# A hybrid decoder layer on one core: old recurrence states as the moving operand, a fourth PSUM place for y, two stores from GpSimd

## The reference

```python
def step(S, inp):
    qc, lfc, kc, vc = inp
    b = jnp.cumsum(lfc, axis=2)
    o_inter = jnp.einsum('bhtd,bhde->bhte', qc * jnp.exp(b), S)
    ...
    o = o_inter + jnp.einsum('bhts,bhse->bhte', A, vc)
    ...
    return S, o
```

```python
o = rmsnorm(o, out_g.reshape(HG_HEADS, HG_DV))
o = o * jax.nn.silu(hg.astype(jnp.float32).reshape(B, T, HG_HEADS, HG_DV))
```

## Time and profile before

| | us |
|---|---|
| median of three runs | 1187.14 (1183.54, 1187.14, 1187.34) |
| profiled execution, its time | 1183.51 |
| profiled execution, its span | 1181.7 |
| PE busy | 1137.4 (96%) |
| DVE busy | 571.8 (48%) |
| ACT busy | 442.9 (37%) |
| GpSimd busy | 354.6 (30%) |
| mean granted clock of TensorE | 0.991 |

### The profile page before, as it was taken

How to read it: one execution, slowest core, us unless ns; L and a number is a source line. 1 busy time by engine, 2 the same in 40 slices (tenths; PEclk the granted TensorE clock), 3 DMA queues, 4 the chain that set the end, 5 groups by cost and what they waited for, 6 DMA issues and landing times.

```text
span 1181.7 us, 20633 instructions
## 1 busy us (share of the span) xinstructions
PE 1137.4 (96%) x8955; PEld 1018.9 (86%) x8955; DVE 571.8 (48%) x788; ACT 442.9 (37%) x737; POOL 354.6 (30%) x226
## 2 busy tenths in 40 slices
PE   5999999999999999999999999999999999999997
PEld 4997564456799999889999877999999999999997
DVE  5533354767436664576622444854444444512332
ACT  6433455667452125222631343243333344311211
POOL 1332100210333163252033101433344444434441
PEclk9999999989999999999999999999999999999999
DMA  5443320420715251224673533323222232313311
GB/s 189 129 141 108 105 92 1 143 73 1 245 65 161 72 177 46 72 80 135 214 286 104 205 148 118 104 72 105 75 90 90 76 104 72 108 63 99 98 63 76
DMA packets 91394, 130.13 MB, mean 110 GB/s; under 512 B 6677, under 2 KB 78729, under 8 KB 89001
## 3 DMA queue, kind: packets, MB, share of 16 engines
q1 hardware_dynamic: 83448, 101.71, 26.3%
q0 software_dynamic: 7856, 27.11, 6.9%
HBM read 120.38 MB, written 12.59 MB: 113 GB/s over the span
## 4 chain that ended last, share of the span: by engine, by line
PE 87%; DVE 5%; ACT 3%; DMA 2%; issue 1%; SPq 0%; DVEq 0%; ACTq 0%
PE ring L742 47%; PE hold L844 6%; PE ring L714 5%; PE ring L1238 2%; PE ring L1437 2%; PE ring L1153 2%; PE ring L1252 2%; PE ring L939 2%; PE ring L950 2%; PE hold L970 1%; PE ring L789 1%; DMA arena<-in_cache_mem_v 1%; PE ring L1500 1%; PE ring L1386 1%; PE ring L1464 1%
## 5 line engine op out<-in xcount | busy, mean ns | idle before, releaser
L633 POOL TENSOR_TENSOR weight_lo<-w_ring,weight_hi 128x1024 fp32r<-128x1024 f32 (+1 forms) x108 | 264.0, 2445 | 551.7 <-ACT weight_hi L1705 551.6
L1705 ACT ACTIVATE weight_hi<-w_ring 128x1024 fp32r<-128x1024 f32 (+1 forms) x135 | 140.4, 1041 | 434.4 <-PE ring L742 358.6
L742 PE MATMUL ring<-operand_hi,weight_hi 128*128 128x272 f32 (+1 forms) x1056 | 219.2, 289 | 0.3 <-ACT arena L2008 0.3
L742 PE MATMUL ring<-operand_lo,weight_hi 128*128 128x272 f32 (+1 forms) x1056 | 218.7, 288 | 0.0
L742 PE MATMUL ring<-operand_hi,weight_lo 128*128 128x272 f32 (+1 forms) x1056 | 217.6, 287 | 0.0
L742 PEld LDWEIGHTS ring<-operand_hi,weight_hi 128*128 128x128 f32 (+1 forms) x1056 | 164.6, 187 | 3.9 <-issue 2.8
L742 PEld LDWEIGHTS ring<-operand_hi,weight_lo 128*128 128x128 f32 (+1 forms) x1056 | 164.7, 187 | 0.4
L742 PEld LDWEIGHTS ring<-operand_lo,weight_hi 128*128 128x128 f32 (+1 forms) x1056 | 164.5, 187 | 0.4
L844 PE MATMUL hold<-arena,w_ring 128*128 128x504 f32 (+1 forms) x192 | 77.2, 521 | 1.2 <-DVE arena L2376 1.2
L1685 ACT ACTIVATE arena<-ring 128x1024 f32<-128x1024 f32 (+8 forms) x75 | 55.5, 748 | 55.5 <-PE ring L742 16.7
L2829 DVE TENSOR_TENSOR x_res<-x_res,ring 128x544 f32<-128x544 f32 x24 | 17.3, 721 | 119.8 <-PE ring L742 119.5
(11 more groups left out here) (441 smaller groups left out, 2185.3 us busy)
## 6 DMA issues: line engine op xcount, KB each, us to landing
w_ring<-in_w_in SPq DMA_DIRECT2D x13, 1024.0 KB, 5.3
w_ring<-in_ffn_w_gate SPq DMA_DIRECT2D x11, 1024.0 KB, 5.3
w_ring<-in_ffn_w_up SPq DMA_DIRECT2D x11, 1024.0 KB, 5.3
w_ring<-in_ffn_w_down SPq DMA_DIRECT2D x8, 1024.0 KB, 5.1
arena<-in_cache_mem_k SPq DMA_DIRECT2D x6, 1024.0 KB, 8.4
arena<-in_cache_mem_v SPq DMA_DIRECT2D x5, 1024.0 KB, 12.1
w_ring<-in_ca_wk SPq DMA_DIRECT2D x4, 1024.0 KB, 5.1
w_ring<-in_ca_wv SPq DMA_DIRECT2D x4, 1024.0 KB, 5.4
```

Source lines behind the costliest of these rows:

```text
L633: self.ops.tensor_tensor(half_of(WL, self.x, kk, cols), w, half_of(WH, self.x, kk, cols).bitcast(F32), ALU.subtract).then_inc(sem("weights ...
L742: last = mm(ps[0:cols, hf * 512:hf * 512 + HALF], half_of((WH, WL)[pw], x, KT, cols)[:, i, :], (xh, xl)[px][:, k, hf * HALF:(hf + 1) * HAL ...
L1705: fn(half_of(WH, y, kk, cols), w, COPY).then_inc(sem("weights_hi"), 1)
```

## The change

Samples: `sample_outputs` on PE is new and runs before `hg_output(0)`. It makes the queries the stationary operand and the old states the moving one. For each head and sequence the stationary block has 32 columns, one per sample token, in which only the 4 columns of the sequence hold queries and the others zeros; DVE writes these blocks in `state_queries` (a memset and four copies into the free buffer `hK`). All 32 + 4 matmuls add up in `HOLD`, 32 rows by 512 columns, a new entry `so` of `hold`. ACT copies them to `orows`, and `hg_output` ends with one transpose of the head's 128 columns into the item, in the place of the nine matmuls.

Order: on ACT the last gate's sigmoid goes ahead of the four `mixed_hi`, on DVE `out_gate(3)` and `gates_ready` go ahead of the four `mixed_lo`. The squares of the memory rows go one head earlier on ACT; their scaling on DVE goes from ahead of `out_taken(3)` to behind the mean square of the outputs.

End: tile 2 of y goes to `HOLD`, and GpSimd issues the stores of tiles 1 and 3.

```diff
+Y_HELD = 2
...
-        item("y", tt)
+        if tt != Y_HELD:
+            item("y", tt)
...
-    hold += [("As",), ("osum",)] + [("rows", h) for h in range(HH)]
-    hold += [("dSs", h) for h in range(HH)] + [("cS",), ("cO",)]
+    hold += [("As",), ("so",), ("osum",)] + [("rows", h) for h in range(HH)]
+    hold += [("dSs", h) for h in range(HH)] + [("cS",), ("cO",), ("y",)]
...
+            def sample_outputs():
+
+                open_hold(("so",))
+                pe.wait_ge(sem("values_in"), 2)
+                pe.wait_ge(sem("state_queries"), HH)
+                for h in range(HH):
+                    hs = slice(h * HK, (h + 1) * HK)
+                    pe.wait_ge(sload[h], 16)
+                    for b in range(DB):
+                        mm(HOLD[0:NSMP, hs], qby[h][:, b, :], S0[:, h, b * HK:(b + 1) * HK],
+                           start=(h == 0 and b == 0), stop=False, skip_group_check=True)
+                    last = mm(HOLD[0:NSMP, hs], AS_[0:NSMP, h, :], hi[0:NSMP, QT, hs], start=False, stop=True,
+                              skip_group_check=True)
+                last.then_inc(hold_full, 1)
+
             def hg_output(h):
...
-                pe.wait_ge(sload[h], 16)
...
-                for b in range(DB):
-                    mm(ps[:, 512 + DS * b:512 + DS * b + DS], S0[:, h, b * HK:(b + 1) * HK],
-                       hQ[:, h, SEQ + DS * b:SEQ + DS * b + DS], start=(b == 0), stop=False, skip_group_check=True)
-                mm(ps[:, 512:TOK], hi[0:NSMP, QT, hs], AS_[0:NSMP, h, :], start=False, stop=True,
-                   skip_group_check=True).then_inc(psum_full, 1)
+                pe.wait_ge(hold_free, hold[("so",)] + 1)
+                tr(ps[:, 512:TOK], orows[:, hs], ident[0:NSMP, 0:NSMP]).then_inc(psum_full, 1)
...
-                evac(act, key)
-                sigmoid(hG[:, h, :], sem("gate_sigmoid"))
...
+            act.wait_ge(hold_full, hold[("so",)] + 1)
+            fn(orows, HOLD[0:NSMP, 0:HH * HK], COPY).then_inc(hold_free, 1)
             for h in range(HH):
                 out_squares(h)
-                if h == 2:
+                if h == 1:
...
+            def state_queries():
+
+                full(dve, ("klT", HH - 1))
+                step(v.memset(hk_flat[:, 0:HH * 256], 0.0))
+                for h in range(HH):
+                    cp(qdiag[h], hQ[:, h, SEQ:TOK].rearrange("p (b t) -> p b t", b=DB)).then_inc(
+                        sem("state_queries"), 1)
+
             state_scan(0)
+            state_queries()
             out_gate(2)
             state_scan(1)
+            out_gate(3)
+            dve.sem_inc(sem("gates_ready"), 1)
             for f in range(4):
                 mixed_lo(f)
-            out_gate(3)
-            dve.sem_inc(sem("gates_ready"), 1)
...
-            for m in range(2):
-                ts(mst[:, m, :], mst[:, m, :], mrs[:, m:m + 1], None, ALU.mult).then_inc(sem("mem_scaled"), 1)
             out_taken(3)
...
             dve.sem_inc(sem("mean_in"), 1)
+            for m in range(2):
+                ts(mst[:, m, :], mst[:, m, :], mrs[:, m:m + 1], None, ALU.mult).then_inc(sem("mem_scaled"), 1)
             refine(RSTD[:, :], MEAN[:, :], hsc)
...
+            for tt in range(1, QT, 2):
+                evac(pool, ("y", tt))
+                g.dma_start(out["y_prompt"][0, tt * P:(tt + 1) * P, :], ymid[:, tt, :]).then_inc(sem("pool_stored"), 16)
+            pool.wait_ge(sem("pool_stored"), 16 * (HH + 1 + QT // 2))
```

More of the change, by code:

```diff
@@ L459, in build @@
         Vbd = SQN.rearrange("p (s n) -> p s n", s=2)
+        hk_flat = hK.rearrange("p h t -> p (h t)")
+        qby = [hk_flat[:, 256 * h:256 * h + 256].rearrange("p (b t) -> p b t", b=DB) for h in range(HH)]
+        qdiag = [hk_flat[:, 256 * h:256 * h + 36 * DB].rearrange("p (b n) -> p b n", b=DB)[:, :, 0:DS] for h in range(HH)]
+        orows = hK[0:NSMP, 3, 0:HH * HK]
         osmp, orow = hsc[0:NSMP, 0:NSAW], SQN[0:NSMP, 3 * SEQ:4 * SEQ]
@@ L1338, in hg_sum @@
                     open_hold(("osum",))
-                    pe.wait_ge(sem("values_in"), 2)
                 pe.wait_ge(sem("o_squares"), h + 1)
@@ L1390, in out_rows @@
                     last.then_inc(sem("half_used") if k else psum_full, 1)
+            sample_outputs()
             hg_output(0)
@@ L1648, in _ @@
             for tt in range(1, QT + 1):
-                final_rows(open_item(("y", tt)), tt, range(KT)).then_inc(psum_full, 1)
+                if tt == Y_HELD:
+                    final_rows(open_hold(("y",)), tt, range(KT)).then_inc(hold_full, 1)
+                else:
+                    final_rows(open_item(("y", tt)), tt, range(KT)).then_inc(psum_full, 1)
         class Steps:
@@ L2012, in _ @@
                     keys_to_rows(3)
+                evac(act, key)
+                sigmoid(hG[:, h, :], sem("gate_sigmoid"))
                 if h == HH - 1:
@@ L2036, in _ @@
                         act.wait_ge(sem("mem_squares"), m + 1)
+                if h == 2:
                     rsqrt(mrs, msm)
@@ L2140, in _ @@
                    COPY).then_inc(sem("crossed_hi"), 1)
-            act.wait_ge(hold_free, len(hold))
+            act.wait_ge(hold_free, hold[("cO",)] + 1)
             act.sem_inc(sem("act_phase"), 1)
@@ L2171, in _ @@
                 key = ("y", tt)
+                if tt == Y_HELD:
+                    act.wait_ge(hold_full, hold[("y",)] + 1)
+                    fn(ymid[:, tt, :], HOLD[:, :], COPY, scale=rs5[:, tt:tt + 1]).then_inc(hold_free, 1)
+                    continue
                 full(act, key)
@@ L2781, in state_new @@
                 dve.sem_inc(sem("state_new"), 1)
-            for h in range(3):
+            for h in range(2):
                 out_taken(h)
@@ L2787, in _ @@
             dve.sem_inc(sem("mean_in"), 1)
+            out_taken(2)
             refine(mrs, msm, mtm)
-            for m in range(2):
-                ts(mst[:, m, :], mst[:, m, :], mrs[:, m:m + 1], None, ALU.mult).then_inc(sem("mem_scaled"), 1)
             out_taken(3)
@@ L3107, in state_out @@
                 g.dma_start(out["s_hgrn"][0, :, h].rearrange("b d e -> d b e"),
-                            S0[:, h, :].rearrange("p (b e) -> p b e", b=DB)).then_inc(sem("hg_stored"), 16)
+                            S0[:, h, :].rearrange("p (b e) -> p b e", b=DB)).then_inc(sem("pool_stored"), 16)
             for n in range(2):
@@ L3121, in _ @@
             g.dma_start(out["p_hgrn"][0, 0].rearrange("h d e -> d h e"), Sst[:, :, QT - 1, :]).then_inc(
-                sem("hg_stored"), 16)
+                sem("pool_stored"), 16)
             for h in range(HH):
@@ L3130, in _ @@
                 state_out(h)
-            pool.wait_ge(sem("hg_stored"), 16 * (HH + 1))
+            pool.wait_ge(sem("pool_stored"), 16 * (HH + 1))
             pool.sem_inc(sem("store_phase"), 1)
@@ L3308, in _ @@
                 weights(c)
-            for tt in range(QT + 1):
-                evac(sp, ("y", tt))
+            for tt in range(0, QT + 1, 2):
+                if tt == Y_HELD:
+                    sp.wait_ge(hold_free, hold[("y",)] + 1)
+                else:
+                    evac(sp, ("y", tt))
                 if tt < QT:
@@ L3315, in _ @@
                 sp.dma_start(dst, ymid[0:n, tt, :]).then_inc(sem("y_out"), 16)
-            sp.wait_ge(sem("y_out"), 16 * (QT + 1))
+            sp.wait_ge(sem("y_out"), 16 * (QT // 2 + 1))
 _OUTS = [("y_prompt", (1, SEQ, DM)), ("y_sample", (DB, DS, DM))]
```

## The result

Over ten executions of each, the changed kernel took 1192.28 us in the median, the kernel before 1186.44: a ratio of 1.0053, 95% interval 1.0033 to 1.0072, so some 6.3 us slower (3.9 to 8.5). Forecast was 1183.7. (One of the ten executions of the changed kernel took 6252.7 us; the median hardly feels it, no other execution in this study did the like, and it stays unexplained.)

A forecast was written before the change was run, and what follows sets the result against it. PE's row of work, 87% of the chain, and the tail behind it were taken as the bound. PE's terms sum to -1.7 us, all else 0: 1185.4 - 1.7 = 1183.7 us, range 1181.0 to 1187.2.

The forecast's parts named there:

- the fourth place and GpSimd's stores: Tail: tile 2 in `HOLD`, tiles 1 and 3 stored by GpSimd; taken as 0, bounds -1.0 and +1.5 us.
- Short products out and the clock of head 1: PE, `hg_output`: dropping 4-column products saves 8.66 us; head 1's seven products at full clock save 1.50 us.
- `sample_outputs`, 8.0: PE, new stage before the heads: 36 matmuls at 0.222 us each add 8.0 us.
- Transposes, 0.45: PE, end of each head: four added transposes at 0.11 us each cost 0.45 us in all.
- Sum on PE: PE's terms together: -8.66 - 1.50 + 8.0 + 0.45 = -1.7 us; without the clock term -0.2.
- The clock holds: PE, 466.8 to 488 us: clock stays 1.00 without short products, worth 1.50 us; chance it doesn't 0.11.
- Two levels: Whole execution: times fall on two levels, 1183.5 and 1187.2 us; the middle, 1185.4, taken as the base.
- more falls are avoided: Rival at the other heads: the higher level comes from further clock falls, also removed, giving 1181.8 us every time; chance 0.23.
- Queries, memory squares, scalings: DVE and ACT: query blocks and earlier squares cost nothing; the two scalings take 2 x 0.75 = 1.5 us.
- The root, at no cost: DVE before `rows_of_norm`: refinement starts 2.3 us behind the mean, costing nothing; rival of it late, 1185.3 us, chance 0.08.
- The tail full at 400 GB/s, so the sooner tile 4 is worth nothing: Program end: tile 4 ready about 1176.3 instead of 1177.36, but transfers stay full behind the first store; 0 us.
- Slower: Rival: `sample_outputs` runs at low clock, 15.8 us, total 1191.5; chance 0.06, plus 0.02 for late store and refinement; 0.08.

The follow-up runs named there:

- after_nowait: Changed kernel, but SyncE instead of GpSimd waits at the end for GpSimd's two stores; gap from first store to end 11.9 us, ratio 1.0033 to the kernel before.
- before_wait: Kernel before, all stores on SyncE, but GpSimd waits at its end for all five; gap from first store to end 15.3 us, ratio 1.0067.
- mid_only: Changed kernel with only its middle kept: result tiles in three places, all stores on SyncE; median 1180.09 us, ratio 0.9982 to the kernel before.
- tail_only: Kernel before with only tile 2 of y put in `HOLD`, all stores on SyncE; gap from first store to end 7.4 us, ratio 1.0008.
- before_drain: Kernel before; GpSimd, its work over, drains between two small writes, then waits for the five stores; drain 7.8 us, gap 7.5 us, ratio 1.0011.

## Why the prediction was wrong

The step that failed is the fourth place and GpSimd's stores, "I take 0", with +1.5 as its upper bound. The bound asked when the last store would land, and for that it was about right: the end of the transfers came some 0.8 us later behind the first store than before (7.8 against 7.0), and with the long drain out of the way the gap is 1.0 us longer (8.4 against 7.4). The Trainium skill (DMA: Bandwidth & Descriptors, section "Issuing engine by pattern") speaks for SyncE; the rows agree, with 5.3 us to landing for GpSimd's two stores and 2.9 for SyncE's. But the end of the program was taken as the last landing. It is the later of two: the last landing plus 0.4 us, or GpSimd's arrival at its closing plus its drain (0.1 + 0.082 x the number of its DMAs) plus 0.4 us. (`after_nowait`, whose drain comes right behind an issue, ended some 1.2 us later than this says.) Before, GpSimd was through near 1162 and its 7.8 us ended near 1170, covered by 11 us of other work; this cover appears in no row ahead of the prediction. The change took it away: 94 + 2 DMAs are 8.0 us, behind the last landing near 1180.0, which with 0.4 for the barrier gives 1188.4, against a span that ended at 1188.3. The prediction asked of every step what hides it, but not of the wait that GpSimd was given at its end.

Point by point:

- *Short products out and the clock of head 1*: old heads took 3.68, 5.40, 3.78 and 3.78 us, 16.64 in all, as read. Right for that execution.
- *`sample_outputs`, 8.0*: 8.78. The eight products of a head take 1.87 us, 0.233 each (0.222 taken), and the closing one, with the step to the next head's stationary, 0.33 (467.66 to 468.00). Mis-sized by 0.8.
- *Transposes, 0.45*: a head costs 1.93 us, 0.36 more than its seven products' 1.57 where 0.11 was taken. The transpose itself is 0.17 (476.34 to 476.51); the rest is the wider step from and to it (0.32 for steps that take 0.22 within the products). Mis-sized by 1.0.
- *Sum on PE*, -1.7 for the profiled execution: 8.78 + 4 x 1.93 = 16.50 against 16.64, -0.1.
- *The clock holds*: right. It is 1.00 in the stage in all six profiles with the new products. The Trainium skill's rule (TensorE: Matmul & The Clock Gate, section "Why this matters for your kernels") looks for idle gaps; the windows of `before_wait` show 5.00 of 5.00 us busy at a clock of 0.50, so it doesn't cover this case.
- *Two levels*: wrong. Ten executions of the kernel before lie between 1182.4 and 1191.7 us, neighbours at most 2.3 apart. What varies is, at least in part, how often and how long the clock falls, in this stage and, untouched by the change, near 165 and 250 us (between 245 and 255 it fell to between 0.50 and 0.66 in four of the sixteen profiles and stayed at 1.00 in the other twelve). So the rival *more falls are avoided* was partly right, and it is what `mid_only` gains from: a mean over executions, which the one profile, with one fall, could not give.
- *Queries, memory squares, scalings*: right; the two scalings took 1.42 us together.
- *The root, at no cost*: nearly. The refinement started 2.56 us behind the mean, not 2.3, and ended at 492.78; PE went on at 492.98, 27.18 us behind the stage's start (27.23 before). The cushion of 0.2 us was the time from the root's end to PE's start, which is 0.2 in both kernels. PE's last step ahead of it took 0.50 us (0.38 before), so the root cost PE 0.1 more than before.
- *The tail full at 400 GB/s, so the sooner tile 4 is worth nothing*: right in the result (`tail_only`). But there the last issue itself moved by only 0.2 us, so a whole 1.0 us of it was not tried with SyncE alone.
- *Slower* had 0.08, for a low clock in the new stage. The side was right and the mechanism was not: the new stage held its clock, and the 8.6 us came in a place that no rival named.

## What to carry to other kernels

Ask of every engine when it comes to its closing, and what its closing costs; GpSimd's has a drain that grows with the DMAs it has issued since its last one, and it is free only while other work covers it. If GpSimd must do something late, let it drain where it idles before (one line, 8 us here), or leave late stores and waits to SyncE. And where the clock falls in some executions only, judge an edit by several profiles of the stage: a single one can price it wrongly in either direction.

## What the runs showed of the hardware

- A drain of GpSimd took 0.1 us behind no DMA, 0.29 behind 2, 2.00 behind 23 and 7.82 behind 94, all of them landed; right behind the issue of four it took 6.6 behind 71. The timelines don't show it: it is idle time there, and the waits credit it at the end of the program to PE's sequencer. The view of its own line has it, as an instruction of GpSimd's queue.
- In the program's closing the same drain took 0.047 us behind none (`before_drain`), 0.217 behind 2, 7.745 behind 94, 7.827 behind 95 and 7.908 behind 96.
- ScalarE arriving last at the closing cost nothing (7.5 us gap), GpSimd arriving last 7.8 us.
- A store of 127 partitions from SyncE moved at 26 GB/s, a DMA share of 0.06, where the stores of 128 partitions kept the DMA at some 400.
- The same TensorE code, busy without a gap, ran its stage in 25.7 to 31.9 us by the granted clock; with the 32 products of 4 moving columns and the 4 of 32 replaced by products of 128, in 27.17 or 27.18 us every time.
